# Transposing x chunk by chunk at the cross-attention and feed-forward norms, with the token's factor applied behind the product

## The reference, cut to what matters

```
h = h + concat(a, c) @ w_out                                  # mixing layer, "out2" in the kernel
h = h + cross_attention(rmsnorm(h, g_cross), rmsnorm(mem, g_mem), wq, wk, wv, wo)
        # q = n @ wq, 4 heads of 128; softmax(q k^T / sqrt(128)) v, then @ wo
nm = rmsnorm(h, g_mlp)
h = h + square(relu(nm @ w1)) @ w2                            # hidden width 8192
rmsnorm(x, g) = x * rsqrt(mean(x*x) + 1e-6) * g               # one factor per token, one gain per column
```

## Time and profile before

| what | value |
|---|---|
| median of 3 runs | 3361.25 us (3359.84 to 3367.35) |
| the profiled execution's own time | 3361.25 us |
| its span, first to last instruction | 3359.3 us |
| mean granted TensorE clock | 0.989 |
| busy: PE, PEld, VectorE, ScalarE, GpSimd | 97%, 88%, 60%, 41%, 2% |
| chain that ended last | PE 88%, DVE 8%, ACT 2%, issue 1% |

### The profile page before, as it was taken

The page is one execution under the profiler, slowest core; times in us unless marked ns, Lnnn a source line. Parts: engine busy times, 40 slices in busy tenths (PEclk is TensorE's granted clock), DMA queues, the critical chain, the costliest instruction groups (busy, mean ns, idle before and its releaser), DMA issues.

```text
span 3359.3 us, 53122 instructions
## 1 busy us (share of the span) xinstructions
PE 3242.0 (97%) x21120; PEld 2951.0 (88%) x21120; DVE 2008.5 (60%) x2827; ACT 1366.7 (41%) x1289; POOL 50.7 (2%) x63
## 2 busy tenths in 40 slices
PE   6999989999999999999999999999897899999998
PEld 6898879999889898999989898899776889999896
DVE  4665449999745555555555465597754555555554
ACT  4463343367333333333333334434334433333332
POOL 0000000000100000000000000000000000000000
PEclk9999999999999999999999999999998999999999
DMA  5433344456755555565656555454442455555553
GB/s 188 176 139 113 115 172 153 163 201 226 249 195 195 203 196 202 193 206 194 206 189 227 202 188 187 157 189 151 153 160 101 162 188 187 187 187 186 188 185 127
DMA packets 85305, 603.54 MB, mean 180 GB/s; under 512 B 9528, under 2 KB 9552, under 8 KB 13904
## 3 DMA queue, kind: packets, MB, share of 16 engines
q1 hardware_dynamic: 77184, 562.07, 47.2%
q0 software_dynamic: 5712, 23.21, 2.6%
q10 hardware_dynamic: 2304, 16.78, 1.3%
HBM read 583.13 MB, written 18.89 MB: 179 GB/s over the span
## 4 chain that ended last, share of the span: by engine, by line
PE 88%; DVE 8%; ACT 2%; issue 1%; DMA 0%; POOL 0%; DVEq 0%; SPq 0%; POOLq 0%; ACTq 0%
PE bank L1444 15%; PE bank L1445 15%; PE bank L1446 15%; PE bank L1469 13%; PE bank L1470 13%; PE bank L1471 13%; DVE w_lo L845 3%; PE bank L1725 2%; ACT w_hi L495 1%; PE bank L1496 1%; PE bank L1532 1%; DVE tmp L1008 1%; DMA raw<-stream_dram 0%; ACT junk_late L536 0%; DVE top_i L1122 0%
## 5 line engine op out<-in xcount | busy, mean ns | idle before, releaser
L845 DVE TENSOR_TENSOR w_lo<-raw,w_hi 128x2048 fp32r<-128x2048 f32 x532 | 1219.5, 2292 | 1041.8 <-ACT w_hi L495 1041.0
L495 ACT ACTIVATE w_hi<-raw 128x2048 fp32r<-128x2048 f32 x532 | 1018.2, 1914 | 907.3 <-PE bank L1471 841.2
L1444 PE MATMUL bank<-a_hi,w_hi 128*128 128x256 f32 x4544 | 1298.7, 286 | 14.1 <-DVE w_lo L845 11.2
L1445 PE MATMUL bank<-a_lo,w_hi 128*128 128x256 f32 x4544 | 1286.8, 283 | 0.0
L1446 PE MATMUL bank<-a_hi,w_lo 128*128 128x256 f32 x4544 | 1286.7, 283 | 0.0
L1444 PEld LDWEIGHTS bank<-a_hi,w_hi 128*128 128x128 f32 x4544 | 872.9, 192 | 20.8 <-issue 12.5
L1445 PEld LDWEIGHTS bank<-a_lo,w_hi 128*128 128x128 f32 x4544 | 873.2, 192 | 0.7
L1446 PEld LDWEIGHTS bank<-a_hi,w_lo 128*128 128x128 f32 x4544 | 872.8, 192 | 0.0
L1469 PE MATMUL bank<-w_hi,a_hi 128*128 128x512 f32 x1728 | 678.0, 392 | 4.3 <-DVE a_lo L1377 3.4
L1470 PE MATMUL bank<-w_lo,a_hi 128*128 128x512 f32 x1728 | 674.5, 390 | 0.0
L1471 PE MATMUL bank<-w_hi,a_lo 128*128 128x512 f32 x1728 | 674.2, 390 | 0.0
(11 more groups left out here) (266 smaller groups left out, 1648.2 us busy)
## 6 DMA issues: line engine op xcount, KB each, us to landing
raw<-stream_dram SPq DMA_DIRECT2D x532, 1024.0 KB, 4.8
gates_scratch<-stage ACTq DMA_DIRECT2D x16, 1024.0 KB, 4.4
gbuf<-gates_scratch POOLq DMA_DIRECT2D x30, 512.0 KB, 5.7
x<-x_dram SPq DMA_DIRECT2D x2, 1024.0 KB, 6.5
mem<-mem_dram POOLq DMA_DIRECT2D x1, 2048.0 KB, 10.2
wide<-wide_dram POOLq DMA_DIRECT2D x2, 1024.0 KB, 5.8
out_dram<-x SPq DMA_DIRECT2D x2, 1024.0 KB, 4.0
keys<-keys_dram POOLq DMA_DIRECT2D x1, 1024.0 KB, 6.0
```

The costliest lines, as they stand in the source:

```text
L495: eng.activation(w_hi[k % SPLIT][:, :], raw[:, k % RAW, :], ACT.Copy).then_inc(hi_done, 1)
L845: eng.tensor_tensor(w_lo[k % SPLIT][:, :], raw[:, k % RAW, :], w_hi[k % SPLIT][:, :].bitcast(F32), ALU.subtract).then_inc(split_done, 1)
L1444: mm(o, hi[:, ks], act_t[0][:, kt, :], start=kt == 0, stop=False)
L1445: mm(o, hi[:, ks], act_t[1][:, kt, :], start=False, stop=False)
```

## The change

The cross-attention norm ("gcross") and the feed-forward norm ("gmlp") no longer write norm. TensorE transposes x itself, four tiles (one chunk of 512 columns) at a time, once the chunk's sum is final:

- gcross: chunks 0, 1 and 2 after out2 units 8, 9 and 12; chunk 3 inside cq unit 0, behind its twelfth tile.
- gmlp: chunks 0, 1 and 2 after co units 1, 2 and 3; chunk 3 inside up unit 0, behind its twelfth tile.

ScalarE and VectorE convert a chunk behind their `ahead` of that unit. The squares of both norms move behind the conversion of chunk 3 on ScalarE. The pairs for cq are built in a2 instead of a1. The factor is applied later: for cross attention as the scale of Exp and in the negated maximum, for the feed-forward layer squared, when the down chunks are added to x. TensorE's first feed-forward round is laid out ahead of the loop.

```
-        BUILT = {n: a2 if n == "gmix" else a1 for n in NORMS}
+        BUILT = {n: a2 if n in ("gmix", "gcross") else a1 for n in NORMS}
# GpSimd
-                eng.tensor_tensor(stat[:, 2:4], stat[:, 4:6], stat[:, 12:14], ALU.pow).then_inc(rs_done, 1)
+                root = eng.tensor_tensor(stat[:, 2:4], stat[:, 4:6], stat[:, 12:14], ALU.pow)
+                if name == "gcross":
+                    own.do(root)
+                    root = eng.tensor_scalar(stat[:, 14:16], stat[:, 2:4], -1.0, None, ALU.mult)
+                if name == "gmlp":
+                    own.do(root)
+                    root = eng.tensor_tensor(stat[:, 14:16], stat[:, 2:4], stat[:, 2:4], ALU.mult)
+                root.then_inc(rs_done, 1)
# ScalarE
                     eng.activation(dst, src, ACT.Exp, bias=amax[:, i % 4, q:q + 1],
+                                   scale=1.0 if a["masked"] else stat[:, 2 + q:3 + q],
-            for j in range(8, 15):
+            for j in range(8, 16):
                 ahead(UNIT0["out2"] + j)
+                if j in (8, 9, 12):
+                    scaled_chunk("gcross", {8: 0, 9: 1, 12: 2}[j])
+            scaled_chunk("gcross", 3)
             eng.wait_ge(resid, 8)
             squares("gcross", x)
-            ahead(UNIT0["out2"] + 15)
-            scaled_tiles("gcross")
...
             for j in range(4):
-                if j == 3:
-                    eng.wait_ge(resid, 10)
-                    squares("gmlp", x)
                 ahead(UNIT0["co"] + j)
-            scaled_tiles("gmlp")
+                if j >= 1:
+                    scaled_chunk("gmlp", j - 1)
+            scaled_chunk("gmlp", 3)
+            eng.wait_ge(resid, 10)
+            squares("gmlp", x)
# VectorE, add_chunk of the down projections (scale = stat[:, 14:16])
-                    eng.tensor_tensor(xs, bank[2 * pair + tt][:, :], xs, ALU.add).then_inc(bank_free, 1)
+                        eng.scalar_tensor_tensor(xs, bank[2 * pair + tt][:, :], scale[:, tt:tt + 1], xs, ALU.mult, ALU.add)\
+                            .then_inc(bank_free, 1)
# VectorE, head_max of cross attention
+                    if i == 0:
+                        eng.wait_ge(rs_done, NQ["gcross"] + 1)
+                    eng.tensor_tensor(amax[:, i % 4, :], amax[:, i % 4, :], stat[:, 14:16], ALU.mult).then_inc(at_max, 1)
# VectorE, out2
-                if j < 15:
-                    ahead(UNIT0["out2"] + j)
-            resid_ready()
-            normalise("gcross", x, norm)
-            scaled_los("gcross")
-            ahead(UNIT0["out2"] + 15)
+                if j == 15:
+                    resid_ready()
+                ahead(UNIT0["out2"] + j)
+                if j in (8, 9, 12):
+                    scaled_lo_chunk("gcross", {8: 0, 9: 1, 12: 2}[j])
+            scaled_lo_chunk("gcross", 3)
# VectorE, co
                 add_chunk(j * 512, j % 2, UNIT0["co"] + j + 1)
+                if j == 3:
+                    resid_ready()
+                ahead(UNIT0["co"] + j)
+                if j >= 1:
+                    scaled_lo_chunk("gmlp", j - 1)
+            scaled_lo_chunk("gmlp", 3)
# TensorE
+            def turn_chunk(name, c, freed):
+                eng.wait_ge(bank_free, freed)
+                for kt in range(4 * c, 4 * c + 4):
+                    turn_tile(name, x, kt)
+            for j in range(8, 16):
...
+                if j in (8, 9, 12):
+                    n = {8: 0, 9: 1, 12: 2}[j]
+                    turn_chunk("gcross", n, out2_free + 2 * n + 2)
+            def last_turn(name, freed):
+                def between(kt):
+                    if kt == 11:
+                        turn_chunk(name, 3, freed)
-                    feature_unit(s, a1, "gcross" if s == 0 else None)
+                    feature_unit(s, a2, "gcross" if s == 0 else None, last_turn("gcross", out2_free + 8) if s == 0 else None)
...
+                if j >= 1:
+                    turn_chunk("gmlp", j - 1, 4 * r0 + 4 + 2 * (j - 1) + 2)
+                feature_unit(j, a1, "gmlp" if j == 0 else None, last_turn("gmlp", b0 + 4) if j == 0 else None)
+            feature("up0", 12, a1, first=4)
+            row_units("down0", 2, a2, None, hidden("up0", None))
+            with eng.Fori(1, FF_ROUNDS) as r:
```

More of the change, by code:

```diff
@@ L533, in square @@
             def square(name, src, tt):
-                junk = junk_early if name in ("ln1", "ln2", "gmem") else junk_late
+                junk = junk_early if name in ("ln1", "ln2", "gmem") else junk_cross if name == "gcross" else junk_late
                 eng.activation(junk[:, :], src[:, tt, :], ACT.Square, accum_out=stat[:, tt:tt + 1]).then_inc(sq_done, 1)
@@ L547, in scaled_tile, with scaled_chunk @@
                     .then_inc(tmp_full, 1)
+            def scaled_chunk(name, c):
+                for kt in range(4 * c, 4 * c + 4):
+                    scaled_tile(name, kt)
             def scaled_tiles(name):
@@ L863, in scaled_lo, with scaled_lo_chunk @@
                                          dst[0][:, kt, :].bitcast(F32), ALU.mult, ALU.subtract).then_inc(tmp_split, 1)
+            def scaled_lo_chunk(name, c):
+                for kt in range(4 * c, 4 * c + 4):
+                    scaled_lo(name, kt)
             def scaled_los(name):
@@ L880, in feature, with add_chunk @@
                     own.leave(n // 4)
-            def add_chunk(c, pair, done):
+            def add_chunk(c, pair, done, scale=None):
                 eng.wait_ge(mm_done, done)
@@ L886, in add_chunk, with row_units @@
                     xs = x[:, tt, bass.ds(c, 512)]
-                    eng.tensor_tensor(xs, bank[2 * pair + tt][:, :], xs, ALU.add).then_inc(bank_free, 1)
-            def row_units(name, pairs, add=True, last=False, r=None, skip=0):
+                    if scale is None:
+                        eng.tensor_tensor(xs, bank[2 * pair + tt][:, :], xs, ALU.add).then_inc(bank_free, 1)
+                    else:
+                        eng.scalar_tensor_tensor(xs, bank[2 * pair + tt][:, :], scale[:, tt:tt + 1], xs, ALU.mult, ALU.add)\
+                            .then_inc(bank_free, 1)
+            def row_units(name, pairs, add=True, last=False, r=None, skip=0, scale=None):
                 u0 = UNIT0[name] + 8 * skip
@@ L894, in row_units @@
                         if add and j % 4 == 3:
-                            add_chunk(lin((j // 4) * 512 + 1024 * skip, (g, 1024)), j // 4, lin(u0 + j + 1, (r, RU), (g, 8)))
+                            add_chunk(lin((j // 4) * 512 + 1024 * skip, (g, 1024)), j // 4, lin(u0 + j + 1, (r, RU), (g, 8)), scale)
                         ahead(u0 + j, (r, RU), (g, 8))
@@ L901, in row_units @@
                         if j % 4 == 3:
-                            add_chunk(loops * 1024 + (j // 4) * 512, j // 4, u0 + 8 * loops + j + 1)
+                            add_chunk(loops * 1024 + (j // 4) * 512, j // 4, u0 + 8 * loops + j + 1, scale)
             def resid_ready():
@@ L935, in head_max @@
                 own.wait()
-                eng.tensor_scalar(amax[:, i % 4, :], amax[:, i % 4, :], -1.0, None, ALU.mult).then_inc(at_max, 1)
+                if a["masked"]:
+                    eng.tensor_scalar(amax[:, i % 4, :], amax[:, i % 4, :], -1.0, None, ALU.mult).then_inc(at_max, 1)
+                else:
+                    if i == 0:
+                        eng.wait_ge(rs_done, NQ["gcross"] + 1)
+                    eng.tensor_tensor(amax[:, i % 4, :], amax[:, i % 4, :], stat[:, 14:16], ALU.mult).then_inc(at_max, 1)
             def head_norm(a, i):
@@ L1423, in _ @@
                 feature("up0", 16, 0, square(r, BQ["up0"]), 8, r)
-                row_units("down0", 2, r=r)
+                eng.wait_ge(rs_done, NQ["gmlp"] + 1)
+                row_units("down0", 2, r=r, scale=stat[:, 14:16])
                 own.leave(FF_ROUNDS - 1)
             feature(f"up{FF_ROUNDS - 1}", 16, 0, square(None, BQ[f"up{FF_ROUNDS - 1}"]), 8)
-            row_units(f"down{FF_ROUNDS - 1}", 2, last=True)
+            row_units(f"down{FF_ROUNDS - 1}", 2, last=True, scale=stat[:, 14:16])
             resid_ready()
@@ L1450, in feature_unit, with feature @@
                         between(kt)
-            def feature(name, n, act_t, r=None, built=None):
-                u0, b0 = UNIT0[name], 4 * ROUND0[name]
+            def feature(name, n, act_t, r=None, built=None, first=0):
+                u0, b0 = UNIT0[name] + first, 4 * ROUND0[name] + first
                 with eng.Fori(0, n // 4) as g:
@@ L1836, in _ @@
                 mix2_unit(s)
-            row_units("out2", 1, a1, skip=1)
-            eng.wait_ge(normed, 10)
-            turn("gcross", norm)
+            def turn_chunk(name, c, freed):
+                eng.wait_ge(bank_free, freed)
+                for kt in range(4 * c, 4 * c + 4):
+                    turn_tile(name, x, kt)
+            out2_free = 4 * ROUND0["out2"] + 4
+            for j in range(8, 16):
+                c = j // 4
+                eng.wait_ge(split_done, UNIT0["out2"] + j + 1)
```

(17 more changed lines are left out.)

1 line of the change is left out of this document (added).

## The result

The changed kernel takes 3344.33 us (median of 5 runs, 3343.03 to 3346.42) against 3359.97 us before (5 runs, 3359.76 to 3367.35). The ratio is 0.9948, with a 95% interval of 0.9935 to 0.9962: half a per cent faster, 15.6 us by the medians and 13 to 22 us by the interval. The profiled execution took 3344.33 us, its span is 3342.1 us. The prediction was 3346 us, a gain of 15.1 us.

A forecast was written before the change was run, and what follows sets the result against it. TensorE, 97% busy, bounds the kernel, so only its waits at the two norms can be won. 8.8 + 7.8 - 1.5 = 15.1 us off 3361.25 us gives 3346 us, 0.45% faster; range 3342.5 to 3352.

The forecast's parts named there:

- the two large terms: Savings behind the last row unit's release: 8.8 us at the cross-attention norm, 7.8 us at the feed-forward norm.
- Part 5: TensorE's clock at both norms: new pauses bring one low stretch, costing 1.5 us; none costs 0, one in each 3.3.
- Chunks between row units: Transposes ahead of row units: each chunk costs TensorE 0.93 us, its conversion nothing; 2.8 us at gcross, 1.9 at gmlp.
- gcross, 8.8 us: Cross-attention norm: scores start 10.9 us behind the last out2 release instead of 22.5; less 2.8 for chunks, 8.8 us saved.
- gmlp, 7.8 us: Feed-forward norm: up unit 2 starts 18.4 us behind the last co release instead of 28.1; less 1.9, 7.8 us saved.
- The scaled add, taken as 0: VectorE's add in the 16 down chunks: at most 0.2 us more, on the path in the last pair alone; 0 to 0.4.
- slower rival: Down chunks: the scaled add delays VectorE's weight split, price 2.35 us each, 25 us in all, 3371 us; chance 0.03.
- The rule that was weighed in the prediction: TensorE at both norms: transposes don't engage the full clock, so both would fall low and the gain be 13.6 us.
- it doesn't overlap: At each turned chunk TensorE stands for a conversion, about 2 us times eight; gain gone, 3355 to 3366 us; chance 0.05.

The follow-up runs named there:

- second trace: The changed kernel run again without an edit: 3345.06 us against 3359.53 us for the kernel before on that chip, ratio 0.9956.
- gcross alone: Changed kernel with the feed-forward norm put back to its earlier form: 3350.8 us against 3363.55 us for the kernel before, ratio 0.9965.
- gmlp alone: Changed kernel with the cross-attention norm put back to its earlier form: 3354.13 us, ratio 0.9974 to the kernel before.
- squares moved: Changed kernel with one of gcross's two squares and both of gmlp's ahead of chunk 3 on ScalarE: 3342.1 us, ratio 0.9938 to the kernel before.
- the factor alone: Changed kernel with no chunk turned during a projection, all 16 tiles turned behind the last add, factor still behind the product: 3346.18 us, ratio 0.9952 to the kernel before.
- the fastest kernel: Changed kernel with VectorE's lo of the last chunks ahead of its weight split and chunk 3 turned earlier: 3338.82 us, ratio 0.9932 to the kernel before.

## Where the prediction held, and the step that failed

The mechanism held: the two large terms came within 0.5 us each, link by link. The step that failed is Part 5, the clock: one low stretch more, -1.5 us. The runs showed +0.3 us in the trace of the result and +0.1 in the second trace.

- **Chunks between row units** (0.93 us each): 6.36 - 5.44 = 0.92 us. Right, from a row of another norm of the same kernel. Their conversion was hidden, as said.
- **gcross, 8.8 us.** Scores 10.5 us behind the release (2539.92 - 2529.42), 10.9 forecast. With three chunks at 0.92 us that is 22.5 - 10.5 - 2.75 = 9.2 us. Each link was there: the pause of 1.60 us for lo, and the squares in front of the cq copy, which one run removed for 1.45 us.
- **gmlp, 7.8 us.** 34.07 - 24.91 - 1.82 = 7.3 us at the full clock, 6.0 in the first trace. At the full clock, in the second trace, the Relu of unit 0 came 2616.39 - 2602.55 = 13.8 us behind the release, 13.5 forecast, and unit 2 started at 18.8, 18.4 forecast.
- **The scaled add, taken as 0.** It takes 0.745 us instead of 0.686, and U to E is 699.55 us with it and 699.59 without it, in the kernel with gcross alone. Hidden in 15 of 16 chunks. The slower rival needed 2.25 us each.
- **The clock, -1.5 us: the step that failed.** It was worked out as one low stretch more at the two norms. In the first trace one did come at gmlp (1.4 us), but another left the first co unit (1.75 us), so the net was +0.3 us. The second trace has neither. The price of a stretch was about right; the count was wrong on both sides. Pauses of 1.60 and 2.04 us at gcross brought no low stretch in three traces (the changed kernel's two and gcross alone), and pauses of 2.2, 1.4 to 1.7 and up to 1.3 us at gmlp brought one in four (the changed kernel's two, gmlp alone, squares moved). On the other side, the low stretch of the first co unit, which the prediction named only as a bound, is gone in four of the six traces with gcross changed (5.8 us for the unit) and there in the other two and in both without (7.4 us). What decides it, no run shows. Without this term the sum would have been 16.6 us against 17.2 of the spans and 15.6 of the medians. That 15.1 is so near the 15.6 is in part luck: the kernel before alone had medians of 3359.97, 3363.55 and 3359.53 us, a scatter larger than the term.
- **Rivals.** Nothing of "it doesn't overlap" or "slower" appeared. What the prediction didn't do is to part the gain between factor and overlap; the run with the factor alone shows that in this order the larger share was in the first. A slip on the side: with one low stretch in each norm, at its own 3.3 us, the gain is 13.3 us and not 13.6.

The rule that was weighed in the prediction can be tested again in that run. Between 2604.9 and 2612.2 TensorE waited and then did nothing but transposes, and the clock fell and rose again in that time:

```profile
2604.90:2607.10 2.20, 0.00 (x0) 0.00 (x0) 2.20 (x3) 0.91 (x3) 0.00 (x0) 0.99 0.25 104
2607.40:2610.50 3.10, 3.10 (x15) 2.57 (x15) 2.85 (x8) 2.52 (x6) 0.00 (x0) 0.51 0.88 277
2610.90:2612.20 1.30, 1.30 (x8) 0.73 (x9) 1.30 (x4) 1.30 (x5) 0.00 (x0) 1.00 0.02 6
```

This is the kernel with the factor alone, in its gmlp turn. The Trainium skill (TensorE: Matmul & The Clock Gate, Part 4: PE-mode transpose) says that the full clock doesn't engage for transposes; by these rows, of fp32 transposes, as by those of before, it does. Nor did the clock fall in both norms, which the prediction drew from that sentence: at gcross no trace with early chunks has a low stretch.

## What to carry to other kernels

Where a norm's only effect on a token is a positive factor, put the factor behind the product first, and turn the raw values as soon as they are final second: here the factor alone brought 12.8 of the 16.6 us that the stretches of the second trace show (12.0 + 9.2 - 1.8 - 2.75), and the early chunks, each paid with 0.92 us of TensorE, only the rest. Then read the brackets behind the last release: what ScalarE and VectorE do there in program order (a sum of squares, a weight split that nobody needs yet) is the price that is left. Putting the conversion ahead of the split, with chunk 3 turned earlier, was worth another 6 us, and raised what the early chunks bring from 3.8 to 10.3 us; so judge an interleaving only after its order has been put right. Cost such a stage as one serial timeline with a clock of its own for each engine, and compare event by event, since the totals scatter by several microseconds.

## What the runs showed that was not expected

- The granted clock doesn't follow from the program at pauses of this length. One and the same program, behind one and the same pause of 2.1 us, ran 3.3 us at 0.51 once and at 1.00 once, and its first co unit began at the full clock in one trace and at the low one in the other. Such stretches move C to A1 between 42.7 and 45.1 us in eight traces whose instructions there are the same but for the factor.
- The time ahead of R scatters too: 2526.96, 2527.91 and 2527.41 us in the three kernels that do the same until then, and 2528.39 to 2532.39 us in the five that turn three chunks. The last of these, 2.4 us above the next, was in the fastest kernel. I didn't look for its cause.
- Exp with its scale read from memory takes 0.56 us for 256 columns, where it took 0.47 us before. It lies beside TensorE's work here, and C to A1 shows nothing of it.
